# Four instead of five rotating buffers for the mixer's weight halves, the fifth pair of buffers given to an expert's half-matrix in the middle of the attention

## The chip, the cores and the metric

One core of a Trainium2 chip runs the program. The metric is the device time of one execution in microseconds; the kernel before takes 1213.95 us (median of 3 runs, 1213.93 to 1214.83). Times inside the kernel are read from one profiled execution, counted from the start of its span.

## What is computed

One decoder layer on 256 tokens of width 1024, all in float32. First the mixer, three branches from one input projection, gated and merged; then a mixture of 32 experts, 4 for each token. Cut to its core:

```python
xn = rmsnorm(h, g_mix); proj = xn @ w_in            # q, k, v, u_pool, q_mem, gate_logits
o = diff_attention(rot(norm(q)), rot(norm(k)), v, lam)      # 8 heads, two softmax maps each
y_attn = subnorm(o) @ w_b_attn
y_pool = multiscale_pool(u_pool, pool_w, pool_scale) @ w_b_pool
y_mem  = memory_cross_attention(q_mem, mem, ...) @ w_b_mem  # 4 heads
merged = g[0] * y_attn + g[1] * y_pool + g[2] * y_mem       # g = sigmoid(gate_logits + b_gates)
h = h + merged @ w_out
h = h + moe(rmsnorm(h, g_ffn), ...)   # per expert: clamped SwiGLU of x@w_gate, x@w_up, then @ w_down
```

The experts' weights are 32 x 3 matrices of 1024 x 1024, 403 MB, and every one is streamed from HBM. The mixer's weights are 22 pieces of 1024 x 512 (46 MB).

## The kernel before, in words

**The mixer's weights.** `PIECES` names the 22 pieces in the order in which they are used: pool, mk, q0, mv, q1, qm, k0, v0, k1, v1, gp0, gp1, wbp, gm0, gm1, wbm, ga0, ga1, wba0, wba1, wo0, wo1. Each is loaded in two halves of 1 MB, H = 2n and 2n + 1 for piece n. Half H goes to buffer `raw{H % HALVES}`; ScalarE copies it, rounded, to `hi{H % HALVES}` (`hi`, L693), and VectorE writes the remainder over the raw half (`lo_whole`, L973). TensorE multiplies with three matmuls instead of one at full precision (L1483; the first two halves go without the split, L1476). So a half needs a load, then ScalarE, then VectorE, before TensorE may read it, and its two buffers are taken until TensorE has read it for the last time.

**Units.** A unit is one piece times one tile of 128 tokens: 24 matmuls. Piece n has the units 2n and 2n + 1 as long as n is below 12; wbp and wbm have four short units each. In the first unit of a piece both halves are read, and in the second again. The first half is therefore free in the middle of the second unit (`first_half_used`), the second half at its end (`unit_done`). `half_free` holds these two waits.

**Where the split stands.** ScalarE and VectorE run their instructions in the order in which they are written. The table `SPLIT_AT` puts the split of half 2n + 3 behind unit 2n, and that of half 2n + 4 behind unit 2n + 1. In `hi_after(u)` the copy stands before ScalarE's own work for unit u (its eviction from PSUM), and between the steps of the attention heads: `hi_after`, then `o_out` of the last head, `exps` of the next, and `aT`, which evicts the weights' transposes. TensorE waits for these with `o_copied` and `at_copied` in `turn_o` (L1637) and `values` (L1626), and for the memory attention's `pt_copied` in `mem_values` (L1563).

**The queue.** All loads of weights are issued from SyncE (SP), which also works in order: `load(H)` first waits for `half_free` of half H - HALVES. For H below HALVES nothing is waited for.

**The experts.** After the mixer the same memory is a ring of 10 slots, 16 KB on every partition, a half-matrix (2 MB) each. Slot 0 lies over the attention's small buffers, slot 3 over `hi4` and `raw4`, slots 5 to 8 over `hi0, raw0` to `hi3, raw3`. `load_half(0, g)` fills slot g for the first pair of experts as soon as what lies there is free: slot 3 after unit 43 (the last that reads half 39, which is in buffer 4), slots 5 to 8 after the halves 40 to 43. From then on a slot is filled again when TensorE has used it. The expert loop (L1773, L1818) is 16 pairs of 12 half-matrices; TensorE waits for each to land.

Of the kernel before, what the change touches and what calls it, by code (L numbers as in the profile page):

```python
# [53 lines left out]
PIECES = ["pool", "mk", "q0", "mv", "q1", "qm", "k0", "v0", "k1", "v1", "gp0", "gp1", "wbp",  # L54
          "gm0", "gm1", "wbm", "ga0", "ga1", "wba0", "wba1", "wo0", "wo1"]
# [7 lines left out]
LAST_PAIR = PER_ROUND - PER_PAIR  # L63
IN_STEPS = 8

HALVES = 5
EARLY = 2
UNITS = []
LAST_UNIT = []
# [114 lines left out]
def decoder_layer(nc, x, mem, mixer_halves, b_gates, pool_w, w_router,  # L184
                  w_gate, b_gate, w_up, b_up, w_down, b_down, table, band, vectors, x_turned, mem_turned, out):
    with ExitStack() as ctx:
# [3 lines left out]
        def sem(name):  # L190
            return ctx.enter_context(nc.semaphore(name))
# [2 lines left out]

        buffers = ("region9", "mem_low", "x_low", "region7", "hi4", "raw4", "region2", "region8", "hi0", "raw0",
                   "hi1", "raw1", "hi2", "raw2", "hi3", "raw3", "region1", "region10",
                   "region0", "region5", "region3", "region4", "region6")
        with nc.sbuf_tensor("experts_ring", [P, RING * 4096], F32) as moe_ring:  # L200
# [68 lines left out]
        def group_cols(u):  # L269

            _, name, t, _ = UNITS[u]
            if name == "mk":
                return stat[:, 8 + MHEADS * t:8 + MHEADS * (t + 1)]
            if name == "qm":
                return stat[:, 16:16 + 2 * MHEADS].rearrange("p (h t) -> p t h", t=NT)[:, t, :]
            half = int(name[1])
            if name[0] == "q":
                return stat[:, 32 + 16 * half:48 + 16 * half].rearrange("p (m t) -> p t m", t=NT)[:, t, :]
            first = (72, 144)[half] + 8 * t
            return stat[:, first:first + 8]  # L280
# [59 lines left out]
        mT_in, cleared = sem("mT_in"), sem("cleared")  # L340
        raw_in = [sem(f"raw_in{i}") for i in range(HALVES)]
        hi_act, lo_ready, first_half_used = (sem(n) for n in ("hi_act", "lo_ready", "first_half_used"))
# [44 lines left out]
        def half_source(H):  # L387

            return mixer_halves[H]

        def raw(H):
            return plain[f"raw{H % HALVES}"][:, :]

        def lower(H):
            return split_of[f"raw{H % HALVES}"][:, :]

        def upper(H):
            return split_of[f"hi{H % HALVES}"][:, :]

        def half_free(engine, H):  # L400

            n, h = divmod(H, 2)
            if h == 1:
                engine.wait_ge(unit_done, LAST_UNIT[n] + 1)
            elif PIECES[n] in ("wbp", "wbm"):
                engine.wait_ge(unit_done, LAST_UNIT[n] - 1)
            else:
                engine.wait_ge(first_half_used, N_FULL[n])
# [3 lines left out]
        def place(g):  # L412

            return g % RING
# [11 lines left out]
        def ring_half(g, size=1):  # L426
            return moe_ring[:, place(g) * 4096:(place(g) + size) * 4096]
# [17 lines left out]
        def _(sp):  # L445
# [5 lines left out]
            def load(H):  # L451
                if H >= HALVES:
                    half_free(sp, H - HALVES)
                sp.dma_start(raw(H), half_source(H)).then_inc(raw_in[H % HALVES], 16)
# [6 lines left out]
            load(3)  # L461
            sp.dma_start(X[:, 0, :], x[0, 0:P, :]).then_inc(x_in[0], 16)
            sp.dma_start(X[:, 1, :], x[0, P:SEQ, :]).then_inc(x_in[1], 16)
            load(4)
            load(HALVES)
            sp.dma_start(MEM, mem[0].rearrange("(t p) n -> p t n", p=P)).then_inc(mem_in, 16)

# [7 lines left out]
            def expert_rows(pair, n):  # L475

                w, e = [(w_gate, 0), (w_up, 0), (w_gate, 1), (w_up, 1), (w_down, 0), (w_down, 1)][n % (PER_PAIR // 2)]
                one = w[bass.ds(pair * 2 + e, 1), :, :].rearrange("e r n -> (e r) n")
                return one.rearrange("(p k) n -> p (k n)", k=KD)

            def load_half(pair, g):

                n, h = divmod(g, 2)
                if g >= LAST_PAIR:
                    landing = last_in[g - LAST_PAIR]
                else:
                    landing = second_in[place(g - 1)] if h else piece_in[place(g)]
                sp.dma_start(ring_half(g), expert_rows(pair, n)[:, h * 4096:(h + 1) * 4096]).then_inc(landing, 16)
# [5 lines left out]
            def biases():  # L494
                for m, b in enumerate((b_gate, b_up)):
                    sp.dma_start(BIAS[m * 2 * EXPERTS:(m + 1) * 2 * EXPERTS, :], b.rearrange("e (h n) -> (e h) n", h=2)
                                 ).then_inc(bias_in, 16)
# [20 lines left out]
            for H in range(HALVES + 1, 2 * N0):  # L518
                if H == 2 * PIECES.index("wba0") + 1:
                    sp.wait_ge(pv_done, HEADS)  # L520
                    biases()
                    sp.wait_ge(merged, 4)
                    load_half(0, 0)
                load(H)
                if H == 2 * PIECES.index("wba1") + 1:
                    sp.wait_ge(oT_done, HEADS)
                    load_half(0, 1)
                if H == 2 * PIECES.index("wo0") + 1:
                    sp.wait_ge(unit_done, UNIT_OF[("ga1", NT - 1, 0)] + 1)
                    load_half(0, 2)  # L530
            sp.wait_ge(unit_done, UNIT_OF[("wba1", NT - 1, 0)] + 1)
            load_half(0, 3)
            sp.wait_ge(mgT_done, 4)
            load_half(0, 4)
            half_free(sp, 2 * PIECES.index("wo0"))
# [1339 lines left out]
```

## Time and profile before

| | us |
|---|---|
| median of 3 runs | 1213.95 |
| profiled execution | 1214.63 |
| its span | 1212.8 |
| TensorE busy | 1169.5 (96%) |
| VectorE busy | 436.5 (36%) |
| ScalarE busy | 260.5 (21%) |

The page gives busy time by engine, a row of 40 slices of 30.3 us each, and the chain of work that ended last. The mixer is the first 300 us: there the 16 DMA engines move 142 to 384 GB/s, and VectorE and ScalarE are busy for up to eight tenths of a slice. From the tenth slice on it is the expert loop, with about 430 GB/s. The granted clock is full (0.99 in the mean). A median of 5.0 us passes from the issue of a 1 MB half to its landing, over the whole kernel.

### The profile page before, as it was taken

The numbers are of one execution on the slowest core, as the hardware profiler recorded it, in microseconds if no ns is written. First come the engines' busy times: TensorE is split into PE (matmuls) and PEld (weight loads), VectorE is DVE, ScalarE is ACT, GpSimd is POOL, SyncE is SP. The second block draws the span as 40 slices with busy tenths as digits, with TensorE's granted clock in tenths as the row PEclk, the third lists the DMA queues.
The fourth block names the chain that finished last, engine by engine and source line by source line (L and its number), as shares of the span: only waits on it lengthen the run. The fifth ranks groups of instructions, "written<-read, shape, count | busy, mean of one in ns | idle before, by whom it ended". The sixth has DMA issues, their size and how long they took to land.

```text
span 1212.8 us, 13717 instructions
## 1 busy us (share of the span) xinstructions
PE 1169.5 (96%) x5436; PEld 581.0 (48%) x5436; DVE 436.5 (36%) x758; ACT 260.5 (21%) x463; POOL 43.7 (4%) x72
## 2 busy tenths in 40 slices
PE   9999999999999999999999999989898989899998
PEld 5888888888434344342434343433333343433342
DVE  5788798665222222222222121212122222221222
ACT  5655477542110110111010001101010101010101
POOL 1321101100000000000000000000000000000000
PEclk9999999999999999999999999999999999999999
DMA  9745645689999999999999999999999999999995
GB/s 384 267 148 185 214 142 186 224 363 394 406 427 431 427 432 432 431 432 431 430 431 430 429 429 432 431 432 431 431 431 432 432 432 431 431 431 431 425 428 232
DMA packets 28172, 460.67 MB, mean 380 GB/s; under 512 B 3216, under 2 KB 3984, under 8 KB 6608
## 3 DMA queue, kind: packets, MB, share of 16 engines
q1 hardware_dynamic: 27008, 456.34, 89.4%
q0 software_dynamic: 960, 3.41, 0.9%
q8 instruction: 49, 0.80, 0.3%
q14 instruction: 11, 0.09, 0.0%
q10 hardware_dynamic: 144, 0.03, 0.0%
HBM read 458.72 MB, written 1.05 MB: 379 GB/s over the span
## 4 chain that ended last, share of the span: by engine, by line
PE 66%; DMA 32%; issue 1%; DVE 1%; POOL 0%; SPq 0%; DVEq 0%; POOLq 0%
DMA experts_ring<-in_w_up 32%; PE bank L1773 25%; PE bank L1483 19%; PE bank L1818 7%; PE bank L1701 5%; PE bank L1761 2%; PE bank L1783 2%; PE bank L1447 1%; PE bank L1476 1%; PE bank L1784 1%; DMA raw<-in_mixer_halves 0%; PE bank L1847 0%; PE bank L1693 0%; PE bank L1602 0%; PE bank L1798 0%
## 5 line engine op out<-in xcount | busy, mean ns | idle before, releaser
L1773 PE MATMUL bank<-experts_ring,region 128*64 128x512 f32 x2048 | 468.4, 608 | 31.9 <-DMA experts_ring<-in_w_gate 21.2
L1773 PEld LDWEIGHTS bank<-experts_ring,region 128*64 128x64 f32 x2048 | 150.2, 139 | 325.5 <-issue 317.5
L1818 PE MATMUL bank<-experts_ring,region 128*64 128x512 f32 x1024 | 228.7, 596 | 2.1 <-DMA experts_ring<-in_w_down 1.9
L1483 PE MATMUL bank<-hi_split,region_split 128*128 128x512 f32 x400 | 151.3, 401 | 0.0
L1818 PEld LDWEIGHTS bank<-experts_ring,region 128*64 128x64 f32 x1024 | 73.6, 137 | 137.6 <-issue 136.4
L1483 PE MATMUL bank<-raw_split,region_split 128*128 128x512 f32 x336 | 130.9, 389 | 0.0
L944 ACT ACTIVATE region<-region 128x512 f32<-128x512 f32 x32 | 20.1, 629 | 452.3 <-DVE region L1409 452.3
L973 DVE TENSOR_TENSOR raw_split<-raw,hi_split 128x2048 fp32r<-128x2048 f32 x42 | 96.1, 2288 | 33.9 <-ACT hi_split L693 33.7
L1417 DVE TENSOR_SCALAR region<-bank 128x512 f32<-128x512 f32 x32 | 22.1, 692 | 236.7 <-PE bank L1784 236.7
L1409 DVE TENSOR_SCALAR region<-bank 128x512 f32<-128x512 f32 x32 | 22.1, 691 | 226.3 <-PE bank L1784 226.3
L1483 PEld LDWEIGHTS bank<-hi_split,region_split 128*128 128x128 f32 x400 | 75.1, 188 | 17.4 <-issue 2.6
L693 ACT ACTIVATE hi_split<-raw 128x2048 fp32r<-128x2048 f32 x42 | 80.1, 1912 | 14.7 <-DMA raw<-in_mixer_halves 14.7
L1432 DVE COPY region<-bank 64x512 f32<-64x512 f32 x32 | 22.2, 694 | 168.7 <-PE bank L1818 168.7
L1483 PE MATMUL bank<-hi_split,x_low_split 128*128 128x512 f32 x208 | 81.2, 390 | 0.0
L1483 PEld LDWEIGHTS bank<-raw_split,region_split 128*128 128x128 f32 x336 | 63.2, 188 | 12.4 <-issue 0.2
L1701 PEld LDWEIGHTS bank<-region 128*128 128x128 f32 x544 | 63.4, 192 | 2.0 <-DVE region L1333 0.5
L1701 PE MATMUL bank<-region 128*128 128x128 f32 x544 | 63.8, 275 | 0.4 <-DVE region L1333 0.4
L1761 PE MATMUL bank<-region 128*128 128x512 f32 x128 | 61.9, 606 | 0.0
L956 ACT ACTIVATE region<-bank 64x512 f32<-64x512 f32 x32 | 18.9, 590 | 152.3 <-PE bank L1818 152.3
L1392 DVE TENSOR_TENSOR region<-bank,region 128x512 f32<-128x512 f32 x68 | 43.9, 685 | 2.4 <-PE bank L1847 2.4
L1483 PEld LDWEIGHTS bank<-hi_split,x_low_split 128*128 128x128 f32 x208 | 39.0, 188 | 8.5
L1783 PEld LDWEIGHTS bank<-extra_split,region_split 128*128 128x128 f32 x64 | 11.9, 186 | 51.9 <-issue 51.9
(183 smaller groups left out, 760.2 us busy)
## 6 DMA issues: line engine op xcount, KB each, us to landing
experts_ring<-in_w_gate SPq DMA_DIRECT2D x26, 4096.0 KB, 36.6
experts_ring<-in_w_up SPq DMA_DIRECT2D x26, 4096.0 KB, 38.8
experts_ring<-in_w_down SPq DMA_DIRECT2D x26, 4096.0 KB, 39.2
raw<-in_mixer_halves SPq DMA_DIRECT2D x44, 1024.0 KB, 5.0
experts_ring<-in_w_up SPq DMA_DIRECT2D x10, 2048.0 KB, 11.1
experts_ring<-in_w_down SPq DMA_DIRECT2D x9, 2048.0 KB, 14.2
experts_ring<-in_w_gate SPq DMA_DIRECT2D x8, 2048.0 KB, 23.3
experts_ring<-in_w_gate SPq DMA_DIRECT2D x8, 1024.0 KB, 9.3
```

What stands on the lines that cost most here:

```text
L693: nc.scalar.activation(upper(H), raw(H), ACT.Copy).then_inc(hi_act, 1)
L973: nc.vector.tensor_tensor(lower(H), raw(H), upper(H), ALU.subtract).then_inc(lo_ready, 1)
L1392: nc.vector.tensor_tensor(X[:, t, h * HALF:(h + 1) * HALF], bank[banks[j]][:, :], X[:, t, h * HALF:(h + 1) * HALF], ALU.add).then_inc(y_ad ...
L1409: nc.vector.tensor_scalar(GS, bank[0][:, :], LIMIT, None, ALU.min).then_inc(g_read, 1)
L1417: nc.vector.tensor_scalar(US, bank[1][:, :], LIMIT, -LIMIT, ALU.min, ALU.max).then_inc(u_read, 1)
L1432: nc.vector.tensor_copy(OE[e * SLOTS:(e + 1) * SLOTS, HALF:D], bank[(2, 1)[e]][SLOTS:2 * SLOTS, :]).then_inc(o_hi, 1)
L1483: ins = nc.tensor.matmul(unit_bank(u)[:, :], a[:, k, toks], b[:, cols], start=(k == 0 and m == 0), stop=(k == k_n - 1 and m == 2))
L1701: ins = nc.tensor.matmul(bank[4 + half][:, b * P:(b + 1) * P], rows_[:, t, (4 * half + b) * P:(4 * half + b + 1) * P], PT[:, t, :], start= ...
L1761: nc.tensor.matmul(bank[6 + j % 2][:, :], PWT[:, t * P:(t + 1) * P], OE[:, h * HALF:(h + 1) * HALF], start=True, stop=True).then_inc(comb_ ...
L1773: ins = nc.tensor.matmul(dst[h * SLOTS:(h + 1) * SLOTS, :], XE[:, kk, e * SLOTS:(e + 1) * SLOTS], w[:, k, h * HALF:(h + 1) * HALF], start= ...
L1783: nc.tensor.matmul(dst[:, :], pick, BIAS_UP, start=False, stop=False)
L1818: ins = nc.tensor.matmul(bank[(2, 1)[e]][h * SLOTS:(h + 1) * SLOTS, :], AHT[e][:, k, half * SLOTS:(half + 1) * SLOTS], w[:, k, h * HALF:(h ...
```

## The change

`HALVES` becomes 4. The names `hi4` and `raw4` become `spare0` and `spare1`: the memory stays where it was, but no mixer half uses it. `load(4)` is no longer issued at the start without a wait; the call of `load(HALVES)` that stands there is now the one for half 4, and waits for half 0. Every later half waits for the release of the half four before it instead of five. Slot 3 of the ring is thereby free from the start, and its half-matrix of 2 MB is issued right behind half 20 (the first half of gp0) instead of after unit 43.

```diff
-HALVES = 5
+HALVES = 4
...
-        buffers = ("region9", "mem_low", "x_low", "region7", "hi4", "raw4", "region2", "region8", "hi0", "raw0",
+        buffers = ("region9", "mem_low", "x_low", "region7", "spare0", "spare1", "region2", "region8", "hi0", "raw0",
...
             sp.dma_start(X[:, 1, :], x[0, P:SEQ, :]).then_inc(x_in[1], 16)
-            load(4)
             load(HALVES)
...
                 load(H)
+                if H == 2 * PIECES.index("gp0"):
+                    load_half(0, 3)
...
             sp.wait_ge(unit_done, UNIT_OF[("wba1", NT - 1, 0)] + 1)
-            load_half(0, 3)
             sp.wait_ge(mgT_done, 4)
             load_half(0, 4)
```

Only SP's instructions move. SP at the start of the kernel before, from the third tile of the start to the halves 5 to 8 (each `raw<-in_mixer_halves` is one half):

```order
9 L454 DMA raw<-in_mixer_halves 128x2048
10 L454 DMA raw<-in_mixer_halves 128x2048 [waits first_half_used]
11 L466 DMA region<-in_mem 128x2x1024
12 L469 DMA tmp<-in_vectors 128x256
13 L470 DMA gqk<-in_vectors 128x128
14 L471 DMA con<-in_table 128x1024
15 L472 DMA region<-in_band 128x2x1024
16 L473 DMA region<-in_pool_w 128x4x128
17 L454 DMA raw<-in_mixer_halves 128x2048 [waits unit_done]
```

The same place of the changed kernel:

```order
9 L454 DMA raw<-in_mixer_halves 128x2048 [waits first_half_used]
10 L465 DMA region<-in_mem 128x2x1024
11 L468 DMA tmp<-in_vectors 128x256
12 L469 DMA gqk<-in_vectors 128x128
13 L470 DMA con<-in_table 128x1024
14 L471 DMA region<-in_band 128x2x1024
15 L472 DMA region<-in_pool_w 128x4x128
16 L454 DMA raw<-in_mixer_halves 128x2048 [waits unit_done]
```

Row 9 was half 4 without a wait, and row 10 half 5; now row 9 is half 4 with the wait that half 5 had, and half 5 is row 16, behind six other transfers and behind the release of half 1.

SP at the end of the mixer before, from half 37 (row 47) to the last first filling of the ring (`experts_ring`):

```order
47 L454 DMA raw<-in_mixer_halves 128x2048 [waits first_half_used]
48 L454 DMA raw<-in_mixer_halves 128x2048 [waits unit_done]
49 L454 DMA raw<-in_mixer_halves 128x2048 [waits first_half_used]
50 L488 DMA experts_ring<-in_w_gate 128x4096 [waits oT_done]
51 L454 DMA raw<-in_mixer_halves 128x2048 [waits unit_done]
52 L454 DMA raw<-in_mixer_halves 128x2048 [waits first_half_used]
53 L488 DMA experts_ring<-in_w_up 128x4096 [waits unit_done]
54 L454 DMA raw<-in_mixer_halves 128x2048 [waits unit_done]
55 L454 DMA raw<-in_mixer_halves 128x2048 [waits first_half_used]
56 L488 DMA experts_ring<-in_w_up 128x4096 [waits unit_done]
57 L488 DMA experts_ring<-in_w_gate 128x4096 [waits mgT_done]
58 L488 DMA experts_ring<-in_w_gate 128x4096 [waits first_half_used]
```

And of the changed kernel:

```order
48 L454 DMA raw<-in_mixer_halves 128x2048 [waits unit_done]
49 L454 DMA raw<-in_mixer_halves 128x2048 [waits first_half_used]
50 L454 DMA raw<-in_mixer_halves 128x2048 [waits unit_done]
51 L487 DMA experts_ring<-in_w_gate 128x4096 [waits oT_done]
52 L454 DMA raw<-in_mixer_halves 128x2048 [waits first_half_used]
53 L454 DMA raw<-in_mixer_halves 128x2048 [waits unit_done]
54 L487 DMA experts_ring<-in_w_up 128x4096 [waits unit_done]
55 L454 DMA raw<-in_mixer_halves 128x2048 [waits first_half_used]
56 L454 DMA raw<-in_mixer_halves 128x2048 [waits unit_done]
57 L487 DMA experts_ring<-in_w_gate 128x4096 [waits mgT_done,unit_done]
58 L487 DMA experts_ring<-in_w_gate 128x4096 [waits first_half_used]
```

Row 56 of before, slot 3, is gone from here (it is now row 32, amid the halves); each half has the wait that the next half had; slots 4 to 9 keep their waits.

## Rows read from the trace of the kernel before

**Rows 1.** Page, slices of 30.3 us: GB/s moved; groups of the two split instructions.

```profile
GB/s 384 267 148 185 214 142 186 224 363 394 406 427 431 427 432 432 431 432 431 430 431 430 429 429 432 431 432 431 431 431 432 432 432 431 431 431 431 425 428 232
...
L973 DVE TENSOR_TENSOR raw_split<-raw,hi_split 128x2048 fp32r<-128x2048 f32 x42 | 96.1, 2288 | 33.9 <-ACT hi_split L693 33.7
...
L693 ACT ACTIVATE hi_split<-raw 128x2048 fp32r<-128x2048 f32 x42 | 80.1, 1912 | 14.7 <-DMA raw<-in_mixer_halves 14.7
```

**Rows 2.** From the waits of PE in the first 305 us: total us, times, longest.

```profile
PE bank L1447 <- DVE prob L1128: 0.6, 1, 0.6
```

**Rows 3.** Chain that ended last: start us, us, what.

```profile
21.16 21.97 PE bank L1483 x96
...
108.29 0.86 PE bank L1563 x4
...
122.75 0.86 PE bank L1563 x4
...
148.51 0.33 PE bank L1615 x3
...
165.49 0.38 PE bank L1637 x2
...
209.57 0.22 PE bank L1637 x2
...
234.10 0.22 PE bank L1637 x2
```

**Rows 4.** The same chain in the expert loop.

```profile
599.57 34.18 DMA experts_ring<-in_w_up
```

**Rows 5.** Windows: us, then busy by engine, clock, DMA share, GB/s.

```profile
20.00:40.00 20.00, 20.00 (x86) 15.88 (x85) 12.21 (x12) 14.18 (x19) 7.31 (x14) 1.00 1.03 410
...
289.50:290.00 0.50, 0.50 (x5) 0.42 (x5) 0.00 (x0) 0.00 (x0) 0.00 (x0) 1.00 0.08 33
```

**Rows 6.** Halves issued from 60 to 225 us: issue to landing.

```profile
DMA to landing us min/median/max: 4.6/4.8/6.1
```

**Rows 7.** Timeline of SP: start us, us, line, what is issued.

```profile
103.40 0.33 SPq L454 DMA_DIRECT2D raw<-in_mixer_halves  x1
...
118.72 0.33 SPq L454 DMA_DIRECT2D raw<-in_mixer_halves  x1
...
132.35 0.33 SPq L454 DMA_DIRECT2D raw<-in_mixer_halves  x1
...
159.26 0.33 SPq L454 DMA_DIRECT2D raw<-in_mixer_halves  x1
...
203.34 0.33 SPq L454 DMA_DIRECT2D raw<-in_mixer_halves  x1
...
231.40 0.33 SPq L454 DMA_DIRECT2D raw<-in_mixer_halves  x1
...
289.29 0.33 SPq L488 DMA_DIRECT2D experts_ring<-in_w_up  x1
```

**Rows 8.** Timeline of ScalarE; in brackets the wait before it, and for what.

```profile
37.57 1.92 ACT L693 ACTIVATE hi_split<-raw 128x2048 fp32r<-128x2048 f32 x1 [3.12 <-DMA raw<-in_mixer_halves]
...
94.22 1.92 ACT L693 ACTIVATE hi_split<-raw 128x2048 fp32r<-128x2048 f32 x1 [0.82 <-DMA raw<-in_mixer_halves]
...
104.71 0.60 ACT L777 ACTIVATE probT<-bank 128x512 f32<-128x512 f32 x1 [1.65 <-PE bank L1447]
...
160.41 1.91 ACT L693 ACTIVATE hi_split<-raw 128x2048 fp32r<-128x2048 f32 x1
...
164.84 0.47 ACT L816 ACTIVATE probT<-bank 128x384 f32<-128x384 f32 x1
```

**Rows 9.** Timeline of VectorE.

```profile
91.64 2.28 DVE L973 TENSOR_TENSOR raw_split<-raw,hi_split 128x2048 fp32r<-128x2048 f32 x1
...
136.03 0.29 DVE L1207 TENSOR_TENSOR prob<-bank,con 128x128 f32<-128x128 f32 x1 [1.31 <-PE bank L1603]
...
147.22 0.48 DVE L1223 SCALAR_TENSOR_TENSOR prob<-prob,stat 128x256 f32<-128x256 f32 x1
```

## The prediction, written before the changed kernel ran

> **What bounds the kernel now.** I read the page's slices first, then the chain that ended last, then the waits of TensorE in the mixer, then SP's, ScalarE's and VectorE's timelines around every load of a half.
>
> The slices show two regimes [rows 1]. In the first 270 us the DMA engines are far from full (142 to 224 GB/s in slices 4 to 8). From slice 12 on they move 425 to 432 GB/s, and the chain runs through the transfers themselves: from 599.57 us on, each pair of experts has a piece of some 34 to 40 us that is the stream of the ring, not TensorE [rows 4]. So the end is set by when the stream's last half-matrix lands. It would be natural to think that 2 MB taken out of this stream is worth 2.1 MB / 430 GB/s = 4.9 us.
>
> In the mixer TensorE is the bound: the chain is nearly all matmuls (96 of them run without a gap from 21.16 to 43.13 us, 5.49 us a unit [rows 3]), and its waits are tenths of a microsecond, the one of note 0.6 us for VectorE at the first memory head [rows 2]. But what TensorE waits for there is often ready only just in time, and that is what the change touches.
>
> **What the moved half-matrix gives: nothing.** It can help only if the queue that it leaves stays busy until the stream is saturated. From 289.50 to 290.00 us the queue moves 33 GB/s [rows 5]: it is empty, with the half-matrix still in its old place. The next one was issued at 289.29 us, when TensorE released half 42 [rows 7]. Everything behind that moment follows the mixer's end, not the bytes issued before. So the 4.9 us turn into a longer gap ahead of 289.3. I take 0; the bounds are 0 and 4.9 us of gain.
>
> **What the fifth buffer costs.** Each half is now issued when the fourth half before it is released. In the kernel before, that release issued the next half, so its time can be read: half H is now issued when half H + 1 was. For a first half (even H) this is the middle of the unit during which ScalarE wants to copy it: ScalarE's `hi_after(u)` stands before its eviction of unit u. The half lands 4.6 to 6.1 us after the issue, in the median 4.8 [rows 6]; I take 4.7 for an idle queue. ScalarE works in order, so it stands until then, with everything behind the copy: evictions, exponentials, the copies that attention on TensorE waits for. The halves themselves still arrive in time for their own matmuls, since 1.9 + 2.3 us for the two split instructions [rows 1] fit into the 5 to 6 us that are left; it is the work behind the wait that is late.
>
> Below, each place is worked on the clock of the kernel before. A stall that has occurred shifts TensorE, the releases and hence the loads by the same amount, so places add up, and the slack at each is counted once.
>
> 1. Start. Half 5 was issued at the first release, ahead of six other transfers. Now it waits for half 1, which is released at 21.16 us, where the chain goes from the first two units to the next [rows 3], and queues behind those six. Half 6, which had this place with one half more in front of it, landed at 37.54 us: ScalarE waited 3.12 us for it [rows 8]. Half 5 lands one 1 MB earlier, at 410 GB/s [rows 5] 2.5 us: at 35.0. Then 1.9 and 2.3 us: 39.2, and 0.1 of handing over. TensorE wants it in the middle of unit 4: 21.16 + 2.5 x 5.49 = 34.9. Stall 4.4 us.
> 2. Memory attention, first head. Half 16 lands at 94.2, when half 17 did before [rows 8], and its copy is done at 96.1. VectorE took it at 91.64 [rows 9] and is from there on busy without a gap until the weights for which TensorE waits already now [rows 2]. All of 96.1 - 91.6 = 4.5 us goes through.
> 3. Half 18: issued at 103.40 [rows 7], + 4.7 + 1.9, then the eviction L777 of 0.6 [rows 8]: 110.6. TensorE's `mem_values` (L1563) stands at 108.29 [rows 3]: 2.3 us.
> 4. Half 20: 118.72 + 4.7 + 1.9 + 0.6 = 125.9, against L1563 at 122.75: 3.2 us.
> 5. Half 22: 132.35 + 4.7 + 1.9 + 2.3 = 141.25, and two small instructions of VectorE, 141.6; the maxima of head 0 began at 136.03 [rows 9]: 5.6 late. The chain from them (maxima, exponentials, half 23, weights) has hardly a gap. The weights were ready at 147.7 [rows 9], TensorE took them at 148.51 [rows 3]: 5.6 - 0.8 = 4.8 us.
> 6. Half 26: ScalarE began its copy at 160.41 and ended `aT` at 165.31, 4.9 us later [rows 8]. Now 159.26 + 4.7 + 4.9 = 168.9, against `turn_o` at 165.49: 3.4 us.
> 7. Half 32, the same in head 5: 203.34 + 4.7 + 4.9 = 212.9 against 209.57: 3.4 us.
> 8. Half 36, after the last head: 231.40 + 4.7 + 1.9, and two evictions of 128 columns, together 0.6 (by the 0.47 of L816 for 384 columns [rows 8]), 238.6 against the last `turn_o` at 234.10: 4.5 us.
> 9. Half 30, and the work of VectorE that half 32 leaves late for head 6: slack there hides most. I take 2.5 us for both, with bounds 0 and twice 3.4.
>
> The other halves are not late: odd ones have their release 2.7 us earlier relative to the use, and where a short piece (wbp, wbm) lies between, the wait has gone. From half 37 on, ScalarE has room, and the last halves (42, 43) are wanted when TensorE has three more units to go.
>
> Sum: 4.4 + 4.5 + 2.3 + 3.2 + 4.8 + 3.4 + 3.4 + 4.5 + 2.5 = 33.0 us. The half-matrix amid this (4.9 us of queue behind half 20) makes half 21 late too, but half 22 behind it is late anyway; 0, at most another 4.9.
>
> From the page "DMA: Bandwidth & Descriptors" of the Trainium skill, "Anatomy of one DMA": a transfer costs about 2.0 us and its bytes at 436 GB/s, a fit made on the other issuing path. For a half that is an estimate of 4.4 us, a little under the trace's 4.6 to 4.8; by it each of seven waits is 0.3 us shorter, and the sum 31. The trace's number is used.
>
> The expert loop keeps its own course: its first loads are released by the end of the mixer, so the whole of it is shifted. Profiled execution: 1214.6 + 33.0 = 1247.6. The runs' median lies 0.7 below the profiled execution: 1247.
>
> **The rivals.**
> - The delays do not add up. Four buffers are still two whole pieces, one in use and one on its way, and neither ScalarE nor VectorE is full in the mixer as a whole. Then only the start's stall remains whole and the others are mostly caught up: 1214 + 4.4 + some of the 28.6, between 1218 and 1234. For it: every half arrives before its own matmuls. Against it: the waits of TensorE are on the work behind the copy, with slacks such as 165.49 - 165.31 = 0.2 and 148.5 - 147.7 = 0.8 us [rows 3, 8, 9] against delays of several us. The Trainium skill's first page ("Trainium Kernel Development and Optimization", Best Practices) says to double-buffer so that transfers lie beside compute; by that rule this change would cost the start alone, 1218.
> - The stream ends earlier. If the queue were never dry, moving the half-matrix takes 4.9 us out of the last stretch, and if the halves are all in time too, the kernel comes to 1209. It decides at one place, the half microsecond before 290, and there rows 5 speak against it; and the start's stall stands against it in any case (together 1213.5, no change).
> - Worse than the sum. If the lateness of ScalarE passes to VectorE and stays there in each head, the slack of item 9 is gone, and if the half-matrix makes half 21 late enough to matter, add 4.9 and twice 3.4: 1259.
> - The change does nothing: SP might be later than the releases already, so that the buffers were never the wait. Against it: an issue takes SP 0.33 us, and its loads stand units apart [rows 7].
>
> **How the numbers follow.** The forecast has 0.80, the worse case 0.05, the catching up 0.10, the stream that ends earlier 0.02, no effect 0.03. The forecast's own range is 1238 to 1256: the landing may be 0.5 us more or less at seven places, and item 9 has its bounds. To leave out no more than 2 in 10 I reach into the catching up: 1234 to 1256. A measurement of this kernel can tell 0.2%, 2.4 us, from no change. Faster 0.03, same 0.03, slower 0.94.
>
> **What would show it.** In the profile after: (a) TensorE waits about 4.4 us in the middle of unit 4, near 35 us; (b) ScalarE's waits for `raw` halves grow from 14.7 us in 8 to over 60 us in more than fifteen; (c) TensorE's waits in the mixer are for ScalarE and VectorE, at L1563, L1615, L1637, 2 to 5 us each, in eight or so places; (d) the first expert product starts near 335 us, and from there to the end it takes as long as before, within 2 us; (e) the queue's gap before the last first fillings is longer than before. The forecast is wrong if TensorE's waits sum to under 20 us, or if the loop after the mixer is shorter by more than 2 us.

## The result, and the profile after

| | before | after |
|---|---|---|
| runs of the comparison, median | 1214.39 us (1213.93 to 1215.11) | 1261.89 us (1261.12 to 1263.02) |
| profiled execution / its span | 1214.63 / 1212.8 | 1261.61 / 1259.8 |
| first expert product begins | 302.32 | 348.75 |
| from there to the end of the span | 910.5 | 911.0 |
| granted clock, mean of the span | 0.99 | 0.977 |

The ratio is 1.0391 (95% interval 1.0373 to 1.0409): 3.9% slower. The forecast was 1247 with a range of 1234 to 1256; the direction was right, the size was not. All of the difference lies ahead of the expert loop.

The windows of each kernel, cut 0.07 us behind the begin of the expert loop (columns as in [rows 5], with the number of instructions behind each busy time). Before:

```profile
0.00:302.39 302.39, 298.19 (x1430) 238.51 (x1432) 223.21 (x354) 166.35 (x273) 43.73 (x72) 1.00 0.66 250
302.39:1212.80 910.41, 871.28 (x4009) 342.54 (x4008) 213.34 (x405) 94.15 (x191) 0.00 (x0) 0.99 0.99 423
```

After:

```profile
0.00:348.82 348.82, 314.14 (x1430) 248.26 (x1432) 223.67 (x354) 166.01 (x273) 47.05 (x72) 0.95 0.57 217
348.82:1259.80 910.98, 870.07 (x4008) 341.19 (x4008) 213.44 (x405) 94.21 (x191) 0.00 (x0) 0.99 0.99 423
```

This is the whole result in two subtractions. In the mixer TensorE's idle time (length less busy) grows from 4.2 to 34.7 us: 30.5 us of new waits, where 33.0 were forecast. And TensorE's busy time grows from 298.2 to 314.1 us for the same 1430 instructions: 16.0 us that the forecast did not have. The column of the granted clock, the third from the end, says what most of them are: 0.95 instead of 1.00. VectorE's and ScalarE's busy times are unchanged.

The page shows it in 40 slices of 31.5 us; the second row answers to [rows 1]. Before, the clock's row had a 9 in every slice.

```profile
PEclk9898998989999999999999999999999999999999
...
GB/s 383 155 196 167 204 120 144 134 208 300 361 413 417 434 427 431 430 432 431 430 430 432 430 431 430 431 432 431 429 432 431 431 431 430 430 431 431 427 425 233
```

TensorE's waits up to 350 us (total, times, longest), where [rows 2] had 0.6 us as the one of note (both kernels have one of 1.3 us in the first microseconds):

```profile
PE bank L1563 <- ACT probT L777: 5.7, 2, 3.3
PE bank L1637 <- ACT probT L816: 4.9, 1, 4.9
PE bank L1637 <- ACT region L835: 4.8, 1, 4.8
PE bank L1483 <- DVE raw_split L973: 4.6, 1, 4.6
PE bank L1637 <- issue: 4.6, 2, 3.6
PE bank L1548 <- DVE region L1074: 3.8, 1, 3.8
PE bank L1602 <- DVE stat L1211: 2.6, 1, 2.6
```

Only one of them, the 4.6 us at L1483, is a unit waiting for its own weights. The others wait for evictions, maxima and rotations of ScalarE and VectorE. (`issue` means that the profile names no releaser; ahead of the longer of these two waits, which ends at 247.42, ScalarE's `aT` ended at 247.31.) What these engines wait for stands in ScalarE's waits over the same stretch. It was 14.7 us in 8 times before:

```profile
ACT hi_split L693 <- DMA raw<-in_mixer_halves: 94.2, 23, 9.1
```

One place in full, head 1 (step 6 of the prediction; it answers to the rows of 160.41 and 164.84 in [rows 8], and 165.49 in [rows 3]): SP's issue, two instructions of ScalarE and one of TensorE.

```profile
185.55 0.33 SPq L454 DMA_DIRECT2D raw<-in_mixer_halves  x1
```

```profile
191.56 1.91 ACT L693 ACTIVATE hi_split<-raw 128x2048 fp32r<-128x2048 f32 x1 [3.91 <-DMA raw<-in_mixer_halves]
...
196.00 0.48 ACT L816 ACTIVATE probT<-bank 128x384 f32<-128x384 f32 x1
```

```profile
196.62 0.66 PE L1637 MATMUL bank<-con,region 128*128 128x128 f32 x2 [4.88 <-ACT probT L816]
```

The half is issued at 185.55 and lands 5.99 us later. ScalarE stands 3.91 us at it and begins the copy 31.15 us later than in the kernel before, `aT` (L816) 31.16 us later. TensorE, which came to this place 26.3 us later than before, waits 4.88 us for `aT`. No work of TensorE at that moment needs the half itself.

The first memory head looks like another such place, but its wait is not the one of the prediction's step 2. ScalarE's copy of half 14, VectorE's split of half 15, VectorE's eviction of the turned keys and queries, TensorE's first scores, and VectorE's split of half 16:

```profile
89.17 1.92 ACT L693 ACTIVATE hi_split<-raw 128x2048 fp32r<-128x2048 f32 x1 [4.91 <-DMA raw<-in_mixer_halves]
...
94.07 2.29 DVE L973 TENSOR_TENSOR raw_split<-raw,hi_split 128x2048 fp32r<-128x2048 f32 x1
...
101.19 1.40 DVE L1074 TENSOR_SCALAR region<-bank,small 128x512 f32<-128x512 f32 x2
...
102.65 3.78 PE L1548 MATMUL bank<-region 128*128 128x256 f32 x8 [3.85 <-DVE region L1074]
...
102.78 2.29 DVE L973 TENSOR_TENSOR raw_split<-raw,hi_split 128x2048 fp32r<-128x2048 f32 x1 [0.19 <-ACT hi_split L693]
```

In the kernel before, the split of half 15 began at 84.54 and L1074 at 90.32. TensorE is 6.7 us later by then, so the split is late by 2.8 us of its own and L1074 by 4.2. The split of half 16 comes only after the wait has ended. The wait at L1447 for VectorE's weights [rows 2], which step 2 saw grow, is gone.

TensorE's other landmarks, which answer to the six times of [rows 3] from 108.29 on, with the wait ahead of each in brackets:

```profile
123.43 0.89 PE L1563 MATMUL bank<-probT,region 128*128 128x256 f32 x3 [2.35 <-ACT probT L777]
141.48 0.89 PE L1563 MATMUL bank<-probT,region 128*128 128x256 f32 x3 [3.33 <-ACT probT L777]
173.97 0.55 PE L1615 MATMUL bank<-con,prob 128*128 128x128 f32 x3 [0.58 <-DVE prob L1223]
...
247.42 0.41 PE L1637 MATMUL bank<-con,region 128*128 128x128 f32 x2 [3.62 <-issue]
278.32 0.69 PE L1637 MATMUL bank<-con,region 128*128 128x128 f32 x2 [4.84 <-ACT region L835]
...
279.23 0.63 PE L1483 MATMUL bank<-raw_split,region_split 128*128 128x512 f32 x1
279.66 0.63 PE L1483 MATMUL bank<-hi_split,x_low_split 128*128 128x512 f32 x1
```

The last rows are what follows a wait: the matmuls of 512 columns begin 0.43 us apart (279.23, 279.66). Before, 96 of them took 21.97 us [rows 3], 0.229 each. They run at 1.2 instead of 2.4 GHz. Windows around two of the waits show the clock's fall and its return:

```profile
35.00:40.00 5.00, 0.57 (x1) 0.50 (x2) 2.29 (x1) 4.10 (x5) 0.63 (x2) 0.69 0.55 228
40.00:45.00 5.00, 5.00 (x16) 3.97 (x15) 2.18 (x2) 4.59 (x6) 3.85 (x11) 0.63 0.00 0
190.00:195.00 5.00, 1.74 (x8) 1.12 (x6) 1.50 (x1) 3.44 (x8) 0.00 (x0) 0.89 0.46 192
195.00:200.00 5.00, 3.38 (x16) 2.61 (x16) 4.24 (x10) 4.33 (x14) 0.47 (x2) 0.50 0.00 2
200.00:205.00 5.00, 5.00 (x26) 4.12 (x25) 4.66 (x10) 3.67 (x10) 0.47 (x1) 0.93 0.20 26
```

From 40 to 45 us TensorE is busy all the time and does 16 matmuls; 5 us at 0.229 each would be 22. In the whole mixer of the changed kernel the granted clock is at the lower level in seven stretches, 37.5 us together; before, in none.

### The profile page after: what moved, and what is told of

Same layout as the page of the kernel before. It is cut to its first block, busy times and chain, and to the rows that moved or that the text cites. A ratio compares the mean times of both kernels' runs of the same rounds, so it can differ in the third digit from the quotient of the medians.

```text
span 1259.8 us, 13718 instructions
## 1 busy us (share of the span) xinstructions
PE 1184.2 (94%) x5436; PEld 589.5 (47%) x5436; DVE 437.1 (35%) x758; ACT 260.2 (21%) x463; POOL 47.0 (4%) x72
## 4 chain that ended last, share of the span: by engine, by line
PE 60%; DMA 34%; issue 2%; DVE 1%; ACT 1%; POOL 1%; DVEq 0%; ACTq 0%; POOLq 0%
DMA experts_ring<-in_w_up 30%; PE bank L1773 25%; PE bank L1483 14%; PE bank L1818 7%; PE bank L1701 5%; DMA raw<-in_mixer_halves 4%; PE bank L1761 2%; PE bank L1783 2%; PE bank L1476 1%; PE bank L1447 1%; PE bank L1784 1%; ACT hi_split L693 1%; DVE raw_split L973 1%; PE bank L1492 0%; PE bank L1548 0%
## 5 line engine op out<-in xcount | busy, mean ns | idle before, releaser
L1483 PE MATMUL bank<-hi_split,region_split 128*128 128x512 f32 x400 | 155.6, 412 | 4.6 <-DVE raw_split L973 4.6
L1483 PE MATMUL bank<-raw_split,region_split 128*128 128x512 f32 x336 | 134.3, 400 | 0.0
L693 ACT ACTIVATE hi_split<-raw 128x2048 fp32r<-128x2048 f32 x42 | 80.3, 1914 | 94.3 <-DMA raw<-in_mixer_halves 94.2
L1483 PEld LDWEIGHTS bank<-hi_split,region_split 128*128 128x128 f32 x400 | 77.8, 195 | 23.7 <-DVE raw_split L973 5.0
L1483 PE MATMUL bank<-hi_split,x_low_split 128*128 128x512 f32 x208 | 84.4, 406 | 0.0
L1483 PEld LDWEIGHTS bank<-raw_split,region_split 128*128 128x128 f32 x336 | 65.7, 196 | 13.3 <-issue 0.2
L1483 PEld LDWEIGHTS bank<-hi_split,x_low_split 128*128 128x128 f32 x208 | 40.9, 196 | 9.2
```

The source lines that it names most:

```text
L693: nc.scalar.activation(upper(H), raw(H), ACT.Copy).then_inc(hi_act, 1)
L1483: ins = nc.tensor.matmul(unit_bank(u)[:, :], a[:, k, toks], b[:, cols], start=(k == 0 and m == 0), stop=(k == k_n - 1 and m == 2))
```

## The experiments

The theory after the comparison has three parts: (A) the moved half-matrix does nothing; (B) TensorE waits for ScalarE and VectorE, which stand in order at a half that has not landed; (C) a wait costs more than its length, because the matmuls behind it run at the lower clock. "First product" is where the mixer's window is cut in the profiled execution, within 0.1 us of the begin of the first expert product (before 302.4, changed kernel 348.8); idle and busy are TensorE's up to there, and "at 1.2 GHz" is how long the granted clock was at its lower level.

| kernel | us (ratio to before, interval) | first product | idle | busy | at 1.2 GHz |
|---|---|---|---|---|---|
| changed kernel | 1261.9 (1.0373 to 1.0409) | 348.8 | 34.7 | 314.1 | 37.5 |
| four_alone | 1261.6 (1.0365 to 1.0397) | 349.7 | 34.2 | 315.5 | 37.5 |
| start_alone | 1221.0 (1.0037 to 1.0064) | 309.4 | 7.8 | 301.6 | 6.8 |
| start_filled | 1219.8 (1.0024 to 1.0052) | 309.1 | 5.5 | 303.7 | 0 |
| all_filled | 1254.0 (1.0303 to 1.0334) | 340.9 | 8.6 | 332.3 | 3.4 |
| start_mended | 1254.9 (1.0319 to 1.0347) | 341.2 | 30.3 | 310.9 | 27.3 |
| last_mended | 1256.9 (1.0339 to 1.0367) | 344.4 | 32.8 | 311.6 | 23.9 |
| safe_five | 1215.3 (1.0000 to 1.0018) | 302.4 | 3.5 | 299.0 | 0 |
| safe_four | 1242.2 (1.0217 to 1.0245) | 329.7 | 23.7 | 306.0 | 10.2 |
| safe_four_more | 1237.0 (1.0169 to 1.0198) | 325.3 | 19.9 | 305.4 | 10.2 |

Three more (late_copies, repaired, late_five) are told below; they can't decide between the causes.

**four_alone: the fifth buffer taken away, the half-matrix left in its old place.**

```diff
                 load(H)
-                if H == 2 * PIECES.index("gp0"):
-                    load_half(0, 3)
...
             sp.wait_ge(unit_done, UNIT_OF[("wba1", NT - 1, 0)] + 1)
+            load_half(0, 3)
```

> Four buffers, but slot 3 of the ring is filled at its old place, after unit 43. Theory (the moved half-matrix neither gives nor costs anything, since the queue is empty near the end of the mixer in both kernels): within 2 us of the changed kernel, 1260 to 1264 us, and the stretch from the first expert product to the end stays at 911 us. Rival 1 (the moved 2 MB shortens the stream): 4.9 us longer than the changed kernel, 1267. Rival 2 (the 2 MB behind half 20 delays the halves 21 and 22 and is part of the unforeseen 13 us): shorter by 3 to 8 us, 1254 to 1259.

1261.6 against 1261.9 us. Moving the 2 MB early neither helps nor harms, to within the 0.2% that can be told; part A holds, for the gain and for the cost.

**start_alone and start_filled: five buffers, and only the start of the changed kernel.** Half 5 waits for half 1 and goes out behind the six other transfers. start_filled adds, in the stall of unit 4, 20 matmuls whose result nobody reads.

```diff
-            load(HALVES)
+            half_free(sp, 0)
...
-            for H in range(HALVES + 1, 2 * N0):
+            half_free(sp, 1)
+            for H in range(HALVES, 2 * N0):
```

```diff
-            unit(4)
+            unit_k(4, 0, 4)
+            for _ in range(20):
+                nc.tensor.matmul(bank[5][:, :], XNT[0][:, 0, 0:P], XNT[0][:, 0:2, :], start=True, stop=True)
+            unit_k(4, 4, KD)
```

> Five buffers as before; only half 5 is issued where the changed kernel has it, behind the release of half 1 and the six transfers. Theory (a wait of TensorE costs its own length and then a stretch of matmuls at the lower clock): a wait of 4.5 us in unit 4, then 6 to 7 us at a granted clock of 0.5, which adds 2 us; +6.7 us, 1221. Rival (a wait costs its length alone, and what exceeded the forecast are waits elsewhere): +4.5 us, 1219.

> As the kernel with the start's stall alone, with 20 matmuls of 128x512 (4.5 us, their product is used by nothing) on TensorE where it would wait. Theory: the granted clock stays at 1.00 and the cost falls to the wait's length, +4.5 to +5 us, 1219, about 2 us less than without them. Rival: the clock has nothing to do with it, the same time as without them or longer.

TensorE's wait in start_alone, and the windows at the stall:

```profile
PE bank L1484 <- DVE raw_split L974: 4.4, 1, 4.4
```

```profile
35.00:40.00 5.00, 0.59 (x2) 0.50 (x2) 2.29 (x1) 4.10 (x5) 0.62 (x2) 0.74 1.00 418
40.00:45.00 5.00, 5.00 (x15) 3.90 (x14) 2.17 (x2) 4.58 (x6) 3.85 (x11) 0.58 0.04 18
```

The same in start_filled, where the clock stays up:

```profile
35.00:40.00 5.00, 5.00 (x23) 3.90 (x23) 2.29 (x1) 3.91 (x5) 0.89 (x2) 1.00 1.00 418
40.00:45.00 5.00, 5.00 (x24) 4.12 (x23) 2.44 (x2) 4.85 (x6) 3.62 (x11) 1.00 0.04 16
```

The start alone costs 6.6 us (1221.0 less 1214.4): 4.4 of wait, as forecast to the tenth, and the rest matmuls at the lower clock. With the clock held up, the 2.1 us are gone from the units behind the stall, but in the profiled execution the kernel has them back as a new wait of 2.0 us for VectorE's rotation (L1552) at the first memory head: half 15 took 7.2 us to land there instead of 4.9. The two kernels' intervals overlap. So one place is too small to price the clock by; inconclusive on C. The new wait is of use for step 2 all the same: it comes with a late half 15, and it is the wait that the changed kernel has at its first memory head (L1548 there).

**all_filled: the changed kernel, with unused matmuls in nine waits** (20, 17, 10, 14, 11, 21, 4, 15 and 20 of them), so that TensorE is busy while it would wait.

```diff
+            fill(14, 17)
             mem_scores(0)
...
                 unit(22 + 2 * h)
+                if h in (1, 4, 5):
+                    fill(23 + 2 * h, {1: 21, 4: 4, 5: 15}[h])
                 if h:
                     turn_o(h - 1)
...
             unit(37)
+            fill(38, 20)
             turn_o(HEADS - 1)
```

> The changed kernel with unused matmuls of 128x512 at nine of TensorE's waits in the mixer, as many as fit into the wait measured there (20, 17, 10, 14, 11, 21, 4, 15, 20). Theory: the waits' 30 us remain, and most of the 15.9 us by which TensorE's matmuls in the mixer took longer goes: 1262 - 13 = 1249 us, range 1246 to 1253, granted clock 1.00 in nearly all of the mixer. Rival (the 15.9 us are not the clock's, or the clock falls whatever TensorE does): 1262 or more.

The window up to the first product, clock 0.99:

```profile
0.00:340.91 340.91, 332.29 (x1562) 264.15 (x1564) 223.19 (x354) 166.20 (x273) 47.30 (x72) 0.99 0.59 222
```

7.9 us less than the changed kernel, though TensorE does 132 matmuls more. At 0.228 us each they are 30 us of the 332.3 busy; the kernel's own work is 302 instead of 314.1: 12 us of the lower clock's cost are gone. Of these, 8 reach the end; the other 4 are in the waits, which with their fillers are 38.7 us instead of 34.7 (8.6 idle and 30.1 of fillers; whether the fillers were a few too many or the waits grew is not separated). 1254.0 is 1 us outside the range that was expected, so less came back than the theory had it. Part C is shown: with the waits together no shorter, the lower clock costs at least 7.9 us of the 16.0.

**start_mended and last_mended: one place of the changed kernel each.** In the first, half 5 is issued ahead of BAND and POOLW, two of the six transfers that stood in front of it; it lands at 30.2 instead of 35.05 us. In the second, ScalarE's copy after unit 37 stands behind the eviction of the last head's output.

```diff
+            load(HALVES + 1)
             sp.dma_start(BAND, band.rearrange("(t p) g n -> p t g n", p=P)).then_inc(band_in, 16)
...
-            for H in range(HALVES + 1, 2 * N0):
+            for H in range(HALVES + 2, 2 * N0):
```

```diff
+            o_out(HEADS - 1)
             hi_after(37)
-            o_out(HEADS - 1)
```

> The changed kernel with one issue moved: half 5 goes out ahead of BAND and POOLW instead of behind them. Its data lands near 30 us instead of 35.05, so TensorE's wait of 4.6 us in unit 4 and the half-clock matmuls behind it (2.1 us) go. If each place is worth its wait and its clock, 1261.9 - 6.7 = 1255.2 us. If only the wait counts and what the clock gives back is taken by the next wait, at the first memory head, 1257.3 us. If start and later places hide each other, 1259 or more.

> The changed kernel with ScalarE's copy of one half (the one after unit 37) put behind its eviction of the last head's output, for which TensorE's last turn_o waits 4.84 us in the changed kernel. Theory (the wait is for ScalarE standing at a half that has not landed, and costs its length and the half-clock matmuls behind it, 6.8 us at half speed, some of them 1.4 us of loss): 1261.9 - 6.3 = 1255.6 us. Rival, only the wait counts: 1257.1 us. Rival, the half itself is late for its matmuls: the wait moves there, 1261 us.

start_mended: 7.0 us less, the wait (4.6) and its clock (2.1). Nothing behind took it back. last_mended: 5.0 us less, below the 6.3 of the theory and nearer the rival. Its waits from 255 us on:

```profile
PE bank L1483 <- DVE raw_split L973: 2.3, 1, 2.3
PE bank L1637 <- ACT region L835: 0.5, 1, 0.5
```

The 4.84 us at turn_o are 0.5, but the next half (37) is now late for its own unit by 2.3: it was issued at 272.8 us behind the biases and the first expert half-matrix, and landed 12.5 us later. In the changed kernel that lateness lay under the wait at turn_o. Two stalls one behind the other cost less than their sum. The shares of this one place are rough: at the stall of unit 4, which the edit leaves as it was, the clock was low for 3.4 us here and for 6.8 us in the changed kernel.

**safe_five and safe_four: four places at once, with a control.** ScalarE's copies in the memory attention go behind the exponentials and evictions that TensorE waits for, VectorE's splits behind the rotations, and the copy after unit 37 behind `o_out`. The heads keep their order. safe_five is the kernel before with this order; safe_four is the changed kernel with this order and half 5 ahead of BAND. A part of the edit (ScalarE, then VectorE):

```diff
-            hi_after(15)
             mem_probT(1)
             mem_exp(2)
+            hi_after(15)
...
+            mem_probT(3)
             hi_after(17)
-            mem_probT(3)
...
-            lo_after(12)
             rotate(12)
             turned_kq(2)
             turned_kq(3)
-            lo_after(13)
+            lo_after(12)
...
             mem_scale(0)
             mem_scale(1)
+            lo_after(13)
             lo_after(14)
```

> Control: the kernel before, five buffers, with only the order of safe_four on ScalarE and VectorE (copies of the halves in the memory attention behind its exponentials and evictions, the copy after unit 37 behind the last o_out; the heads keep their order). If the order costs nothing by itself, 1214 us within 2; if it does, as it did in the heads (VectorE is busy 88% there), above 1218.

> The changed kernel with the order of safe_five and half 5 ahead of BAND and POOLW: four places are mended, the heads are not. Theory (ScalarE stands in order at a half on its way, and each wait costs its length and a part at half clock): 6.7 at the start, 4 at the first memory head, 5.7 at the two mem_values, 6.3 at the last turn_o are gone: 1239 us, 1236 to 1243. Rival (it is the halves themselves that are late, not what stands behind their copies): the waits come back at the units, and only the start's 6.7 go, 1255. TensorE's remaining waits are those for ScalarE and VectorE in the heads, near 175 and 197 us less the mended ones.

The order costs next to nothing by itself (1215.3 us, interval 1.0000 to 1.0018). With four buffers it and the earlier half 5 give 19.7 us back. The waits of safe_four:

```profile
PE bank L1639 <- ACT probT L818: 4.9, 1, 4.9
PE bank L1639 <- issue: 4.5, 2, 3.6
PE bank L1604 <- DVE stat L1213: 3.6, 1, 3.6
PE bank L1485 <- DVE raw_split L975: 2.7, 1, 2.7
PE bank L1550 <- DVE region L1076: 1.4, 1, 1.4
...
PE bank L1565 <- DVE mem_low_split L986: 0.7, 1, 0.7
```

The stall at unit 4 is gone, the first memory head has 1.4 instead of 3.8, mem_values 0.7 and 0.6 instead of 5.7; the waits that remain are the heads', as expected, and the 2.7 us of half 37. Apart from half 5 no load was moved. What was mended is only the order of the work around the copies and splits, and this is part B: of the 19.1 us at the first product, 11.0 are idle time and 8.1 are busy time, the clock's share.

**safe_four_more: two of the remaining ones.** Half 37 ahead of the biases and the expert half-matrix; and in head 1 alone ScalarE's copy behind `aT` and `qkT`, VectorE's split behind `head_weights`.

```diff
                 if H == 2 * PIECES.index("wba0") + 1:
+                    load(H)
                     sp.wait_ge(pv_done, HEADS)
                     biases()
                     sp.wait_ge(merged, 4)
                     load_half(0, 0)
+                    continue
                 load(H)
...
-                hi_after(a)
+                if h != 1:
+                    hi_after(a)
...
                     qkT(h + 2)
+                if h == 1:
+                    hi_after(a)
```

> safe_four (1242.2 us) with two more edits. One: half 37 is issued ahead of the biases and of the first expert half-matrix, behind which it landed 12.7 us after its issue; TensorE's wait of 2.69 us for VectorE near 275 us goes (2.7 and a little clock, 3 us). Two: in head 1 alone, ScalarE copies the half behind the copy of the turned weights instead of ahead of the last head's output, and VectorE splits it behind the next head's weights; TensorE waits 4.91 us there for ScalarE's L818 and some matmuls run at half clock (3.4 us of them, 1.7 of loss). Theory: 1242.2 - 3 - 6.6 = 1232.6 us. Rival (VectorE is so full in the heads that what it does later is late for the next head, as when all heads were changed): part of the 6.6 comes back at the next maxima or turn_a, 1235 to 1242.

1237.0, 5.1 less than safe_four. The theory said 1232.6; the result lies in the rival's range (1235 to 1242), in which VectorE's later work comes back as waits of the next head. Its largest waits:

```profile
PE bank L1649 <- issue: 6.1, 3, 3.6
PE bank L1614 <- DVE stat L1218: 4.2, 1, 4.2
PE bank L1627 <- issue: 1.8, 2, 1.3
```

The 4.9 us for `aT` and the 2.7 us for half 37 are gone from the list; half 37 lands 6.6 us after its issue. In their place stand waits in the heads: 1.6 us more before turn_o (L1649), 0.7 more before turn_a (L1627) and 0.6 more at the scores that need the first maxima (L1614).

**late_copies, repaired, late_five: the edit that was itself the cost.** Before safe_four I had put the copies late in all heads too, behind `exps` and `aT` (late_copies), and with the start and the first memory head mended as well (repaired); late_five has that order on five buffers.

```diff
-                hi_after(a)
-                if h:
                     o_out(h - 1)
...
                 aT(h)
-                gate_exp_of(a)
                 if h + 2 < HEADS:
                     qkT(h + 2)
+                hi_after(a)
+                gate_exp_of(a)
```

> The changed kernel with ScalarE's copies of halves (hi) moved behind the steps that TensorE waits for: behind o_out, exps, aT and qkT in each head, behind the memory heads' copies L777, half 22 behind the exponentials of head 0, half 36 behind the last o_out. Four buffers and all loads stay as they are. Theory (the cost is the work that stands behind an early copy on an engine that works in order): the stalls of the heads and of the later memory heads go with their clock losses, and what is left is the start (6.7 us) and the first memory head (6.3 us): 1214 + 13 = 1227, range 1224 to 1232. Rival (four buffers are too few, the halves come too late for their own matmuls): over 1245.

> The same, and also: half 5 is issued ahead of the last two of the six transfers at the start, and round the first memory head the copies and splits of the halves 15 and 16 stand behind the key and query steps on ScalarE and VectorE. Theory: nearly all of the loss goes, and nothing is gained: 1214 to 1219. Rival (the moved half-matrix does shorten the stream once the stalls are away): under 1212.

> Control: the kernel before, with five buffers, with only the order of ScalarE's copies in the heads and memory heads changed as in late_copies. Theory: nothing waited there before, so it stays within 2 us of 1214. Rival (the old order itself had cost): shorter by more than 2 us.

They took 1270.9, 1261.6 and 1252.2 us (ratios 1.0444 to 1.0479, 1.0365 to 1.0400, 1.0288 to 1.0323). All three expectations were misses (1227, 1214 to 1219, and 1214 within 2). The control alone lost 38 us, so the two others say nothing on four buffers. Where the control lost it:

```profile
PE bank L1614 <- issue: 18.8, 6, 5.5
PE bank L1636 <- ACT probT L816: 4.6, 1, 4.6
```

L1614 is `turn_a`, which needs VectorE's weights. In the heads VectorE's split of the half stood where it had been, ahead of the weights, and now waited for a copy made later; over the mixer these waits were 33.7 us in 16 times before, and in late_five:

```profile
DVE raw_split L972 <- ACT hi_split L693: 71.8, 23, 5.8
```

And VectorE has little slack to make it good, as its 78.81 us in 90 of the kernel before show. ("Up to eight tenths of a slice", ahead of the prediction, is too low for VectorE: the sixth slice of the page, which lies here, has a 9.)

```profile
145.00:235.00 90.00, 89.24 (x468) 72.65 (x467) 78.81 (x154) 63.02 (x147) 10.84 (x21) 1.00 0.48 172
```

## Why the prediction was right and wrong

| step | forecast | wait found | same matmul, before and after | TensorE later by |
|---|---|---|---|---|
| 1 start | 4.4 | 4.6 | 39.12, 45.84 | 6.7 |
| 2 first memory head | 4.5 | 3.8, another wait | 107.90, 120.69 | 6.1 |
| 3 half 18, mem_values | 2.3 | 2.3 | 110.32, 125.69 | 2.6 |
| 4 half 20, mem_values | 3.2 | 3.3 | 129.31, 149.86 | 5.2 |
| 5 half 22, turn_a(0) | 4.8 | 2.6 + 0.6 | 149.34, 175.02 | 5.1 |
| 6 half 26, turn_o | 3.4 | 4.9 | 172.20, 205.18 | 6.7 |
| 7 half 32, turn_o | 3.4 | 3.6 | 222.79, 262.16 | 5.1 |
| 8 half 36, last turn_o | 4.5 | 4.8 | 245.52, 291.95 | 7.1 |
| 9 and the rest | 2.5 | 0.9, 0.5 and small ones | | 1.9 |
| sum | 33.0 | 30.5 by the windows | | 46.4 |

The times are begins of one matmul in both kernels, read behind each wait and behind the slow matmuls that follow it. The last column is how much more TensorE is behind there than at the place above: 149.86 less 129.31 is 20.55, 125.69 less 110.32 is 15.37, which makes 5.2 for step 4. The 0.6 us that come between steps 5 and 6 and the 1.3 between steps 6 and 7 are in the last row.

- **What bounds, and the moved half-matrix: right.** The loop behind the mixer took 0.6 us longer, and four_alone shows 0 for the move. The last first fillings follow the mixer's end: the issue of [rows 7] at 289.29 came at 335.72, 46.4 later.
- **The mechanism: right in the main, wrong at one place.** ScalarE waited 94.2 us in 23 times (over 60 in more than fifteen was named), TensorE at eight places by 2 to 5 us, and the waits add up to 30.5 us. Six of the eight are waits that the prediction had: unit 4, the two `mem_values`, and the three `turn_o`. Step 5 has its wait one instruction earlier than I put it (at the scores, which need the maxima's end, L1602). Step 2 had the wrong one: it counted half 16 and the weights and took the halves 14 and 15 to be in time, but TensorE waits earlier, for the rotation behind those two (L1548). That 3.8 us came near the forecast 4.5 is luck. Step 6 is 1.5 us larger because its half took 5.99 us to land where I took 4.7; the half issued at that moment in the kernel before, 27, took 5.85 too, near the largest of [rows 6], and the median was the wrong choice for it. safe_five and safe_four show that the order behind the copies makes the waits of the memory attention and of the last turn_o. For the heads only one place was tried (head 1), and a part of its 4.9 us came back as other waits; the rest is read from the timelines.
- **The step that failed: the sum.** "A stall that has occurred shifts TensorE ... by the same amount" is not so: the sum prices each wait at its length and the clock at nothing. Behind seven of the eight waits, those from 2.6 us up, matmuls run at 1.2 GHz, and TensorE is later by 1.5 to 2.2 us more than the wait. Only the wait of 2.3 us (step 3) has the full clock behind it and costs hardly more than itself. This term, 16.0 us of busy time, is the whole miss: 33.0 less the 2.5 that the waits came out below it, and 16.0 more, make 46.5. The lower clock explains most of it, not all: in the seven stretches TensorE is busy for 28.7 of the 37.5 us, and half of that is 14.3 (an estimate); the other 1.7 are open (safe_five, with the clock full, has 0.8 more than the kernel before). all_filled takes 7.9 us away with the waits no shorter, and safe_four gives back 8.1 us of busy time beside 11.0 of waits.
- **Could it be seen beforehand?** Not in the mixer of the kernel before, which had no wait above 1.3 us, nor in the clock's row of its page, which had a 9 everywhere. But the expert loop of that kernel holds the price. TensorE waits there for half-matrices, and behind seven waits of 2.5 to 2.6 us the clock is at the lower level for 3.4 us. The waits at that line from 302 us on (total, times, longest), and one of the seven stretches, behind a wait of 2.62 us that ends at 682.52:

```profile
PE bank L1773 <- DMA experts_ring<-in_w_gate: 21.2, 8, 2.8
```

```profile
683.50:686.90 3.40, 3.40 (x12) 1.16 (x10) 0.00 (x0) 0.00 (x0) 0.00 (x0) 0.50 1.07 458
```

I had read the clock as settled because it was full in every slice of the page. The page "TensorE: Matmul & The Clock Gate" of the Trainium skill, "HAM oscillation — how this bites in real kernels", does say that waits for data can throttle TensorE again and again, and puts the cost at half of the throttled time. By that rule the 37.5 us here would cost 18.8 us, an estimate; the trace has 16.0, and for 8.8 us of those stretches TensorE is idle.

- **The rivals.** "The delays do not add up" and "the stream ends earlier" are out by their numbers. "Worse than the sum" (1259) came near in time, but by another mechanism: the half-matrix has no cost, and the waits were smaller than the sum.
- **Open:** how much of the 16.0 us a perfect clock would give back at the end; all_filled bounds it from below at 7.9, and its fillers are no exact fit. A fifth buffer kept beside the early half-matrix was not tried: no room is left for it. No version found beats the kernel before.

## What to carry to other kernels

When a change makes the engine that bounds the kernel wait, price each wait at its length and, in this kernel for the waits of 2.6 us and more, at the slower matmuls behind it (1.5 to 2.2 us a wait; over the mixer half as much again). A page whose clock row is full everywhere can hide such stretches; look at the windows behind the longest waits that the kernel already has. A buffer less in a rotation is not dear where its data is used but where an engine that works in order stands at the load; moving such a copy behind the work that others wait for cost nothing in the memory attention and gave the waits there back; in the heads it was dear. What differs is that the split that uses the copy was moved with it in the first case and not in the second, and that VectorE has little slack in the heads; which of the two decides was not separated. Run the mending edit on the old kernel first: here the same kind of edit was free in one stretch and cost 38 us in another, where VectorE was 88% busy.

## What the hardware showed that was not expected

- TensorE's granted clock fell from 2.4 to 1.2 GHz around single waits of 2.6 to 4.9 us and was back some microseconds later, seven times in one mixer; filled with unused matmuls, the same waits left it at 0.99. Behind some waits it was low for 3.4 us, behind others for 6.8. The same place can differ between kernels: the wait of 2.3 us at step 3 left the clock full in the changed kernel, and in four_alone a wait of 2.4 us there had 3.4 us at 1.2 GHz behind it.
- The landing time of a 1 MB half varies at the same place between kernels: 4.7 to 5.1 us as a rule for the halves 15 and 16, but 7.2 and 6.9 in start_filled; 12.5 us in last_mended for half 37, behind an expert's half-matrix of 2 MB and two small transfers.
